# Feature-major inputs and output, and the modulation sums moved from TensorE ahead of the first FFN to VectorE beside the first two FFNs

## The reference

```
x = x + 0.5 * swiglu(rms_norm(x, g0), w_gate_up, w_down)       # 4 FFNs in all, D_FF = 2816
x = x + stick_breaking_attention(...)   /  sliding_window_attention(...)
...
sc = jax.nn.silu(c);  sctx = jax.nn.silu(c_ctx)                # 1024 values each
for i in range(2):
    shift_x, scale_x, gate_x = jnp.split(sc @ w_mod[i] + b_mod[i], 3, axis=-1)
    shift_c, scale_c, gate_c = jnp.split(sctx @ w_mod[i] + b_mod[i], 3, axis=-1)
    hx = modulate(rms_norm_2(x, norm_g[i]), shift_x[:, None], scale_x[:, None])
    hc = modulate(rms_norm_2(ctx, norm_g[i]), shift_c, scale_c)
    ...attention over ctx (256 rows) and x...
    x = x + gate_x[:, None] * (ox @ w_o[i])
return rms_norm_2(x, final_g)
```

## Time and profile before

| what | value |
|---|---|
| median of 3 runs | 3031.51 us (3030.82 to 3036.52) |
| the profiled execution: its time, its span | 3030.34 us, 3028.5 us |
| TensorE matmul busy, share of the span | 2870.4 us, 95% |
| VectorE busy | 1529.5 us, 51% |
| ScalarE busy | 1147.8 us, 38% |
| GpSimd busy | 110.4 us, 4% |
| DMA over the span | 234.27 MB, mean 77 GB/s |
| mean granted TensorE clock | 0.972 of full |

### The profile page before, as it was taken

The page is one execution under the profiler, slowest core; times in us unless marked ns, Lnnn a source line. Parts: engine busy times, 40 slices in busy tenths (PEclk is TensorE's granted clock), DMA queues, the critical chain, the costliest instruction groups (busy, mean ns, idle before and its releaser), DMA issues.

```text
span 3028.5 us, 38808 instructions
## 1 busy us (share of the span) xinstructions
PE 2870.4 (95%) x14416; PEld 2334.9 (77%) x14416; DVE 1529.5 (51%) x2151; ACT 1147.8 (38%) x1799; POOL 110.4 (4%) x108
## 2 busy tenths in 40 slices
PE   7999999998999999999987899999999997999987
PEld 2588888887888888888866788887788886878876
DVE  2244426665544335442456444424566666367774
ACT  2323215555323224222354332223455555245452
POOL 1000000000000000000011000000101000010100
PEclk9999999999999999999998899999999998999998
DMA  8433322122333233333301133332111110111111
GB/s 306 153 93 99 99 97 60 45 62 56 98 97 97 97 97 88 99 93 103 92 28 29 49 94 101 91 105 75 49 42 42 35 42 21 56 42 29 43 29 63
DMA packets 333666, 234.27 MB, mean 77 GB/s; under 512 B 6952, under 2 KB 308112, under 8 KB 333584
## 3 DMA queue, kind: packets, MB, share of 16 engines
q1 hardware_dynamic: 332672, 231.63, 25.4%
q0 software_dynamic: 912, 1.53, 0.2%
HBM read 231.04 MB, written 2.10 MB: 77 GB/s over the span
## 4 chain that ended last, share of the span: by engine, by line
PE 88%; DVE 5%; ACT 4%; issue 2%; DMA 0%; POOL 0%; ACTq 0%; SPq 0%; DVEq 0%; POOLq 0%
PE ps L439 24%; PE ps L441 24%; PE ps L440 23%; PE ps L732 3%; PE ps L708 2%; PE ps L1067 2%; PE ps L1204 2%; PE ps L956 1%; PE ps L1042 1%; ACT apr L1837 1%; PE ps L835 1%; PE ps L839 1%; PE ps L920 1%; PE ps L1184 1%; DVE tmp L488 1%
## 5 line engine op out<-in xcount | busy, mean ns | idle before, releaser
L439 PE MATMUL ps<-act_h,wl 128*128 128x512 f32 x2224 | 891.5, 401 | 3.6 <-DVE act_l L2037 2.3
L441 PE MATMUL ps<-act_h,wh 128*128 128x512 f32 x2224 | 868.1, 390 | 0.0
L440 PE MATMUL ps<-act_l,wh 128*128 128x512 f32 x2224 | 867.3, 390 | 0.0
L434 DVE TENSOR_TENSOR wl<-raw,wh 128x1024 fp32r<-128x1024 f32 x382 | 461.1, 1227 | 526.5 <-ACT wh L430 521.7
L430 ACT ACTIVATE wh<-raw 128x1024 fp32r<-128x1024 f32 x382 | 392.5, 1051 | 420.8 <-PE ps L441 347.8
L439 PEld LDWEIGHTS ps<-act_h,wl 128*128 128x128 f32 x2224 | 418.7, 188 | 96.1 <-issue 10.6
L440 PEld LDWEIGHTS ps<-act_l,wh 128*128 128x128 f32 x2224 | 419.1, 188 | 89.9 <-issue 7.9
L441 PEld LDWEIGHTS ps<-act_h,wh 128*128 128x128 f32 x2224 | 418.2, 188 | 89.4
L439 PE MATMUL ps<-h_h,wl 128*128 (+1 forms) x704 | 277.4, 394 | 0.0
L441 PE MATMUL ps<-h_h,wh 128*128 (+1 forms) x704 | 276.0, 392 | 0.0
L440 PE MATMUL ps<-h_l,wh 128*128 (+1 forms) x704 | 273.2, 388 | 0.0
(11 more groups left out here) (339 smaller groups left out, 3805.7 us busy)
## 6 DMA issues: line engine op xcount, KB each, us to landing
raw<-in_ffn_w_gate_up SPq DMA_DIRECT2D x176, 512.0 KB, 4.0
raw<-in_ffn_w_down SPq DMA_DIRECT2D x88, 512.0 KB, 3.7
mod_raw<-in_w_mod SPq DMA_DIRECT2D x12, 2048.0 KB, 8.0
raw<-in_a_w_in SPq DMA_DIRECT2D x32, 512.0 KB, 4.1
raw<-in_sb_w_in SPq DMA_DIRECT2D x24, 512.0 KB, 3.9
raw<-in_b_w_in SPq DMA_DIRECT2D x20, 512.0 KB, 4.0
raw<-in_w_o SPq DMA_DIRECT2D x16, 512.0 KB, 4.0
raw<-in_sw_w_in SPq DMA_DIRECT2D x10, 512.0 KB, 4.0
```

Source lines behind the costliest of these rows:

```text
L434: dve.tensor_tensor(wl[:, slot, :], raw[:, slot % RAWS, :], f32(wh[:, slot, :]), ALU.subtract).then_inc(lo_done[slot], 1)
L439: pe.matmul(bank, w_lo, r_hi, start=start, stop=False, skip_group_check=skip)
L440: pe.matmul(bank, w_hi, r_lo, start=False, stop=False, skip_group_check=skip)
L441: return pe.matmul(bank, w_hi, r_hi, start=False, stop=stop, skip_group_check=skip)
```

## The change

- `kernel()` hands x, ctx_2 and the output feature-major (128 x 8 x tokens), and all small vectors, biases, sinks, lambdas and rotary frequencies as one array `columns` (128 x 430). The transposes of setup and end, their PSUM copies and 17 small loads are gone; x goes straight to `x` in 8 loads of 256 KB (2 on SyncE's queue, 6 on ScalarE's), and y out of `yt` in 8 stores of 256 KB, each issued when its `yt[:, k, :]` is there.
- The stage `mod` is gone. `w_mod` comes transposed (output column on the partition, the 1024 inputs along the row) as 96 chunks of 128 x 512, 48 in each of the first two FFNs, issued by GpSimd into two buffers (`wmod`, a part of `xc`). For each chunk VectorE does two `tensor_tensor_reduce` (multiply by the silu row, and sum), one for each condition vector. Three chunks stand in each turn but the first of the gate/up loop, 18 in the down part; VectorE's loops in those two FFNs are written out. The halves are summed, bias added and `gmod` formed in the fourth FFN.
- ctx is loaded after the last chunk of the second FFN, and its squares are summed in the output projection of the sliding-window attention. The lambda exponentials move to the end of the first FFN's loop.
- Other stages' instructions are the same.

```diff
         def _(sp):
...
+            sp.dma_start(columns[:, :], a["columns"]).then_inc(columns_in, 16)
+            for k in range(2):
+                sp.dma_start(x[:, k, :], a["x"][:, k, :]).then_inc(x_in[k], 16)
...
-                if st.kind == "mod":
-                    for n in range(MOD_LOADS):
-                        if n >= MOD_RAWS:
-                            sp.wait_ge(mod_used, START + n - MOD_RAWS + 1)
-                        sp.dma_start(mod_raw[:, n % MOD_RAWS, :, :],
-                                     w_mod[n // 6][:, :, n % 6 * SEQ:(n % 6 + 1) * SEQ]
-                                     ).then_inc(mod_landed[n % MOD_RAWS], 16)
...
-            sp.wait_ge(rows_out, 8)
-            sp.dma_start(y_out[0].rearrange("(b p) d -> p b d", p=P), yrows[:, :, :]).then_inc(out_sem, 16)
-            sp.wait_ge(out_sem, 16)
+            for k in range(KT):
+                sp.wait_ge(xf_done, START + 8 * stages[-2].n["xf"] + k + 1)
+                sp.dma_start(y_out[:, k, :], yt[:, k, :]).then_inc(out_sem, 16)
+            sp.wait_ge(out_sem, 16 * KT)
...
+            def modulation(half_):
+                pool.wait_ge(mod_used, START + half_ * MOD_CHUNKS // 2)
+                for v, name in enumerate(("c_2", "c_ctx_2")):
+                    pool.dma_start(mod_silu[:, v, :], a[name][:, half_ * SEQ:(half_ + 1) * SEQ].to_broadcast([P, SEQ])
+                                   ).then_inc(mod_row_in, 16)
+                for i in range(half_ * MOD_CHUNKS // 2, (half_ + 1) * MOD_CHUNKS // 2):
+                    if i > 1:
+                        pool.wait_ge(mod_used, START + i - 1)
+                    pool.dma_start(mod_w[i % 2], a["w_mod_2"][:, i, :]).then_inc(mod_in[i % 2], 16)
+                if half_ == 1:
+                    pool.wait_ge(mod_used, START + MOD_CHUNKS)
+                    pool.dma_start(xc[:, :, :], a["ctx_2"]).then_inc(ctx_in, 16)
...
             def setup():
...
+                for k in range(2, KT):
+                    act.dma_start(x[:, k, :], a["x"][:, k, :]).then_inc(x_in[k], 16)
+                act.dma_start(kf[:, :], a["shape_table"][:, 0:N_F * P]).then_inc(const_in, 16)
+                act.dma_start(krows, a["shape_table"][:, N_F * P:]).then_inc(const_in, 16)
+                act.wait_ge(columns_in, 16)
+                act.wait_ge(consts_done, 1)
+
+            def first_norm(st):
+                split_hi(act, *half(st.following, 0))
+                for k in range(KT):
+                    act.wait_ge(x_in[k], 16)
+                    act.activation(act_h[:, k, :], x[:, k, :], ACT.Identity,
+                                   scale=vec[:, st.gain + k:st.gain + k + 1]).then_inc(xhi_done, 1)
+                split_hi(act, *half(st.following, 1))
+                for n in range(KT):
+                    square(act, stages[0], n)
+                act.wait_ge(const_in, 16 * 2)
+                act.activation(kr[:, :, :].rearrange("p a b -> p (a b)"), krows, ACT.Copy).then_inc(consts_done, 1)
...
+            def first_norm(st):
+                split_lo(dve, *half(st.following, 0))
+                for k in range(KT):
+                    dve.wait_ge(x_in[k], 16)
+                    dve.nop().then_inc(xup_done, 1)
+                    gained_lo(st, k)
+                split_lo(dve, *half(st.following, 1))
+                for n in range(KT):
+                    add_square(dve, stages[0], n)
...
+                def modulated(n):
+                    i = f * MOD_CHUNKS // 2 + n
+                    if n == 0:
+                        dve.wait_ge(mod_silu_done, f + 1)
+                    dve.wait_ge(mod_in[i % 2], 16 * (i // 2 + 1))
+                    dve.wait_ge(mod_used, START + i)
+                    for v in range(2):
+                        last = dve.tensor_tensor_reduce(mod_w[i % 2] if v else mod_prod, mod_w[i % 2], mod_silu[:, v, :],
+                                                        1.0, 0.0, ALU.mult, ALU.add, mpart[:, f, n, v:v + 1])
+                    last.then_inc(mod_used, 1)
...
                     up_scaled(0, i)
+                    if extra:
+                        modulated(3 * i - 3)
                     gated(0, i)
                     split_lo(dve, *half(st, 4, i))
                     h_lo(0, i)
+                    if extra:
+                        modulated(3 * i - 2)
                     gate_scaled(1, i)
                     split_lo(dve, *half(st, 5, i))
                     up_scaled(1, i)
+                    if extra:
+                        modulated(3 * i - 1)
                     gated(1, i)
                     h_lo(1, i)
...
+                if f < 2:
+                    for t in range(2, 24):
+                        split_lo(dve, *half(st, 2 * FT + t))
+                        if t < 20:
+                            modulated(28 + t)
```

More of the change, by code:

```diff
@@ L178, in make_plan @@
     plan.stage("sw", lead=2, fixed=2, times=4)
-    plan.stage("out", lead=8, w="sw", count=("res",))
+    plan.stage("out", lead=8, w="sw", count=("res", "cres"))
     ffn(1, 1)
@@ L215, in build_program @@
     w_down = [[tiled(a["ffn_w_down"][l, j]) for j in range(2)] for l in range(2)]
-    w_mod = [tiled(a["w_mod_2"][l]) for l in range(2)]
     w_sb_in, w_sw_in = tiled(a["sb_w_in"][0]), tiled(a["sw_w_in"][0])
@@ L665, in _ @@
                         pool.memset(f32(t[:, :, :]), 0.0).then_inc(B.zero, 1)
+                if st.kind == "ffn" and st.n["ffn"] < 2:
+                    modulation(st.n["ffn"])
                 if st.kind == "sw":
@@ L1320, in out_projection @@
                                 ctx_args=(ps[:, 4 + t, 0:CTX], actc_h, actc_l) if st.ctx else None)
-            def end():
-                pe.wait_ge(xf_done, START + 8 * stages[-1].before["xf"])
-                for b in range(NBLK):
-                    for k4 in range(2):
-                        transposes(2 * b + k4, lambda k: yt[:, 4 * k4 + k, b * P:(b + 1) * P],
-                                   4).then_inc(etr_done, 1)
-            for st in stages:
-                if st.kind == "setup":
-                    setup()
-                elif st.kind == "mod":
-                    modulation(st)
-                elif st.kind == "norm":
+            for st in stages:
+                if st.kind == "norm":
                     norm(st)
@@ L1347, in _ @@
                     out_projection(st)
-                elif st.kind == "end":
-                    end()
         @block.scalar
@@ L1400, in norm @@
                     if st.before["res"] == 1:
-                        for k in range(KT):
-                            gained_hi(st, k)
+                        first_norm(st)
                     return
@@ L2042, in norm @@
                     if st.before["res"] == 1:
-                        for k in range(KT):
-                            gained_lo(st, k)
+                        first_norm(st)
                     return
@@ L2683, in out_projection @@
                 add_square(dve, st, KT - 1)
+                if st.w == "sw":
+                    first_ctx_add(dve, KT - 1)
                 if st.ctx:
                     add_square(dve, st, KT - 1, "c")
[L2687 to L2690 removed]
             for st in stages:
```

280 lines of the change are left out of this document (119 added, 161 removed).

## The result

The changed kernel takes 2937.8 us (median of four runs, 2937.45 to 2943.52) against 3034.0 us before: a ratio of 0.969, 95% interval 0.967 to 0.971. It is faster by 3.1%; forecast were 2920.0 us, 2913 to 2932. The profiled execution took 2937.45 us and its span is 2935.4 us, against 3030.34 and 3028.5 us before, so the spans differ by 93.1 us where the prediction summed 111.5.

The account below looks back on a forecast made before the run. TensorE was taken as the bound, with 88% of the span and 115.67 us ahead of the first FFN matmul. Gains of 102.5 + 9.4 - 0.4 = 111.5 us gave 2920.0 us, range 2913 to 2932.

Parts of the forecast that it names:

- The landing of half 0: Start of the first FFN: the first weight half lands at 9.8 us if the queues share evenly.
- A: Moment when ScalarE starts the high part of the first weight half: taken as 10.0 us, bounds 8.4 and 15.07.
- rival B: Head starved by late loads: 5.1 us less gain, up to 9 with a wait, 2925 to 2930 us; chance 0.15.
- A + 3.2: First FFN's first matmul, about 3.2 us after ScalarE starts splitting the first weight half: forecast at 13.2 us.
- The third floor: Arrival of x blocks as a limit on the first split's start: called not binding, block 7 read 5.4 us after.
- The mean: TensorE's mean in the first FFN: squares ready 0.5 us ahead, no wait charged, up to 1 us kept.
- rival E: Shorter low clock after the start: at most 2.9 us more gain, total under 2916 us; chance 0.03.
- The sums: 192 multiply-and-sums on VectorE in the first two FFNs: 0.75 us each, 144 us in all, charged at nothing.
- Rival D: Slower than before because VectorE's sums become the bound: gain eaten at 2.56 us per sum; chance 0.03.
- Rival C: VectorE or chunk loads cost TensorE hidden time: 2930 to 2950 us, about 2970 if always late; chance 0.11.
- No changed duration of any stage: Sign of being wrong: a changed duration of any stage from the stick-breaking attention on.
- The end: Stores of y issued as each part is done: end comes 9.4 us sooner, between 6.7 and 10.0.

Follow-up runs that it names:

- Experiment 4: Changed kernel with GpSimd's first four chunk loads (1 MB) held back until the first FFN's activations are split: 2932.8 us.
- experiments 5 and 8: 5: SyncE issues all of x behind half 0, changed kernel: 2939.2 us; 8: GpSimd issues ScalarE's eight loads, on 32 bytes, held loads, half 0 first: 2918.0 us.
- experiment 6 with the early table load alone: Changed kernel with 32 unused bytes ahead of the stage tensors and ScalarE's table load ahead of its waits, GpSimd's loads not held: 2923.4 us.
- experiments 1 to 3: Unused bytes ahead of the stage tensors: changed kernel with 32, 2924.8 us; 96, 2933.7; 160, 2939.7; kernel before with 64, 3047.7; 704, 3029.5.
- experiment 1: Changed kernel with 32 unused bytes ahead of the stage tensors, which puts `h_h` at byte 138624: 2924.8 us.
- the 32 bytes: Changed kernel with 32 unused bytes ahead of the stage tensors, nothing else: 2924.8 us.
- The kernel before, at the same address: Kernel before with 704 unused bytes ahead of the stage tensors, which puts `h_h` at byte 138624: 3029.5 us.
- the 32 bytes and the held loads: Changed kernel with 32 unused bytes and GpSimd's first chunk loads held back until the first FFN's activations are split, table load not moved: 2916.1 us.

## Why the prediction was wrong

The mechanism was right, and its largest number was 92% right. The total missed the range by 6 us. Two steps failed; had either of them held, the total would have been inside the range. By the prediction's own steps, in spans:

| step | forecast | measured |
|---|---|---|
| first FFN matmul sooner | 102.5 | 94.6 |
| up to the mean, then the loop | 0 | -0.8 |
| down parts of four FFNs | 0 | -8.4 |
| other stages, moved ctx work | -0.4 | -4.4 |
| the end | 9.4 | 12.1 |
| sum | 111.5 | 93.1 |

**The landing of half 0 failed** (A at 17.85 instead of 10.0 us; 6.6 of the 7.9 us). The step is "if the queues share evenly, some 2.5 MB have moved when half 0 is in: 0.75 + 2.5 x 3.6 = 9.8 us". It landed at 16.55, when 4.6 MB had moved. What the prediction called its rival B, with "half 0 lands with the last of the 4 MB, at 15.07 us or somewhat after", is what the head did, at the price given there (5.1 us, up to 9 with a wait at the mean; measured 7.9 + 0.8). Experiment 4 shows that GpSimd's four loads make the difference: without them 8.25 us. The prediction had put them into the sum as bytes, but charged them by an even share. The share was even by packets: from 9 to 12 us SyncE's queue got 0.10 of 1.07 MB.

**The table load was put on the wrong side of the wait.** The prediction counted it in the floor of A that comes from ScalarE's issues, hidden behind the loads. In the program it belongs to the first activation and comes after the wait for half 0: that is the other 1.3 of the 7.9 us.

**A + 3.2 held**, 3.19 us. **The third floor held** in the changed kernel, where no x block was waited for, and broke as soon as half 0 was put ahead (experiments 5 and 8).

**The mean**: the squares were to be ready 0.5 us ahead; TensorE waited 0.70 us for their sum, which was done at A + 14.7, not 13.7. The prediction followed ScalarE, and ScalarE was ready for the squares in time. But VectorE's low split of half 1 stands ahead of its sums, and ScalarE's third square had to wait for them:

```profile
27.10 0.64 ACT L469 ACTIVATE tmp<-x 128x512 f32<-128x512 f32 x1 [1.31 <-DVE tmp L481]
```

The margin was called thin, and up to 1 us kept for it. The same chain takes away what rival E hoped for. In the changed kernel the first matmuls stand 0.43 us apart for 5.3 us, where they did so for 5.7 before. In the kernel of experiment 6 with the early table load alone they do so for 3.1 us only, and the mean still comes 11.70 us behind the first matmul: a shorter low stretch there gives back nothing, since TensorE waits for the squares.

**The sums** were mis-sized on the safe side, 0.61 us for 0.75, and are hidden in the loop, as charged. Rival D needed 2.56 us. Rival C asked for waits of TensorE on `wl` or of VectorE on chunks in the FFNs; behind the first half there is one row of that kind, 0.2 us of VectorE. GpSimd's issues beside a busy VectorE took 3.1 to 3.4 us to land, as the 3.3 of the earlier trace rows: no sign of the wait for the descriptors.

**"No changed duration of any stage" failed.** The prediction counts a changed duration from the stick-breaking attention on among the signs of being wrong, and its sum has no term for it. The tacit argument was that the same instructions take the same time. The 8.4 us in the down parts are shown to come from where the stage tensors start, `h_h` and `h_l` in these parts (experiments 1 to 3); the change replaced `ssq_c`, `vec`, `lam4` and others by `wmod`, `columns` and `mpart`, and so moved them by 672 bytes. The 0.7 us ahead of the second FFN go the same way (50.9 to 51.0 us at remainders of 0 and 96, 50.3 at 192, 49.9 at 128, in both programs). Ahead of the fourth FFN it is another thing: the changed kernel needs 51.2 us at each of its four remainders, the kernel before 49.9 at the address of experiment 1. With the 32 bytes TensorE waits there 1.06 us for the low part of the last activation block:

```profile
1652.36 0.50 PE L435 MATMUL ps<-act_h,wl 128*128 128x512 f32 x1 [1.06 <-DVE act_l L1996]
```

The kernel before, at the same address, has no such wait. What stands there in addition are the moved squares of ctx, 0.40 us of ScalarE and 0.42 of VectorE behind each block: the term of 0.4 us was 1.4 by this comparison, inside its bound of 2. No run left the squares out.

The 1.8 us of the sliding-window stage are a matter of the clock. TensorE stands idle in it for 46.8 us in both kernels (45.9 to 47.1 us in all fourteen profiles of this case), and is busy 169.6 instead of 167.7 us. The difference arises in the stage's second 20 us, before and after:

```profile
1510.85:1530.85 20.00, 18.16 (x76) 13.40 (x74) 11.65 (x16) 9.60 (x14) 3.36 (x2) 1.00 0.24 68
1424.48:1444.48 20.00, 18.14 (x70) 13.41 (x69) 11.69 (x16) 9.64 (x14) 3.36 (x2) 0.91 0.22 63
```

Why the clock is low there in the one and not in the other is not settled.

**The end** was too small by 2.7 us. A 256 KB store took 2.1 us to land, not the 3.3 of a load of that size on GpSimd's queue, and the last one did not queue: 1.7 of the 2.7. The row was a load on GpSimd's queue, the store goes by SyncE's. The other 1.0 is the mean's two matmuls at full clock. It is luck: in six of the ten other changed kernels, that of experiment 1 among them, they took 2.07 or 2.08 us as before.

The estimate of 2.6 us from the Trainium skill (DMA: Bandwidth & Descriptors, "Anatomy of one DMA"), which the prediction weighed and put aside, was nearer than the row. But the page's sum is for transfers of GpSimd's kind, as the 3.3 us was; neither the 2.1 us nor the 6.6 of the 2 MB store that the prediction found in agreement is one.

With the 32 bytes and the held loads, the two things that failed are undone: 2916.1 us, ratio 0.9622 (0.9606 to 0.9638), against a forecast of 2920. Four us of that are a gift of the address, which is better than that of the kernel before. The fair partner is the kernel before at the same address, 3029.5 us: 113.4 us less, where 111.5 were forecast.

## What to carry to other kernels

When a change adds or drops a buffer, print the start addresses of the tensors that TensorE streams, before and after, and compare the mean duration of the same matmuls: here unused bytes moved the kernel by 13 us either way. A load that the first instruction waits for is not safe at the head of its own queue: hold back what other queues can do without, count the bytes of all queues, and look at the size of the pieces: here each queue got as many packets as the others, so the one with the smallest pieces got the fewest bytes. The table load stood here with the activation that needs it, behind its wait; look for it in the trace between the wait and the work.

## What the runs showed of the hardware

- A matmul with a moving operand of 128x512 fp32r took 389, 388 to 394, or 395 to 396 ns in the profile with a start of the operand at 128, 192, or 0 and 96 by remainder of 256 bytes, all at a granted clock of 1.00. The starts of neighbouring matmuls were 0.227, 0.229 and 0.234 us apart. Four starts were tried from one program and three from the other, six addresses in all; 128 was met at one address. Why is open, as is whether the stationary side's address counts.
- 1 MB in four loads of GpSimd's queue delayed one 512 KB load of SyncE's queue by 8.3 us, while all 16 engines moved up to 375 GB/s.
- Busy queues got equal or nearly equal numbers of packets: 204, 204 and 182 from 9 to 12 us, 578 and 578 from 12 to 16 us. The queue with the 512-byte pieces thus got 0.10 of 1.07 MB and 0.30 of 1.46 MB.
- ScalarE took 0.58 to 0.79 us for each DMA issue of x (3.50 to 4.75 us for six), against 0.45 us for each of SyncE's two ahead of them (0.90 us).
- The sliding-window stage took 213.3 to 219.7 us, as its mean granted clock was 0.88 to 0.84, with 45.9 to 47.1 us of idle time of TensorE in all of them.
